# Spreading the second halves of crowded experts evenly over the units that have an empty half

## What is computed

```python
expert_id = g_top * MOE_PER_GROUP + top_i
gate = jnp.sum(jax.nn.one_hot(expert_id, MOE_EXPERTS, dtype=f32) * w[..., None], axis=1)
hid = jax.nn.silu(jnp.einsum('nd,edf->nef', hf, w_gate)) * jnp.einsum('nd,edf->nef', hf, w_up)
y = jnp.einsum('nef,efd->nd', hid * gate[:, :, None].astype(hid.dtype), w_down)
```

```
layer 0:  49 56 21 64  4 11 13 12 143 124 79 40 142 129 57 80
layer 1:  73 92 74 141 9  5  8  8  14  10 13 19  68 171 73 246
```

## Time and profile before

| | us |
|---|---|
| median of the three runs | 1496.72 |
| the profiled execution | 1495.05 |
| span of its trace | 1493.3 |
| TensorE matmul busy | 1313.4 (88%) |
| VectorE busy | 607.2 (41%) |
| ScalarE busy | 389.9 (26%) |
| GpSimd busy | 302.8 (20%) |

### The profile page before, as it was taken

How to read it: one execution, slowest core, us unless ns; L and a number is a source line. 1 busy time by engine, 2 the same in 40 slices (tenths; PEclk the granted TensorE clock), 3 DMA queues, 4 the chain that set the end, 5 groups by cost and what they waited for, 6 DMA issues and landing times.

```text
span 1493.3 us, 21495 instructions
## 1 busy us (share of the span) xinstructions
PE 1313.4 (88%) x7940; PEld 842.8 (56%) x7940; DVE 607.2 (41%) x1513; ACT 389.9 (26%) x815; POOL 302.8 (20%) x290
## 2 busy tenths in 40 slices
PE   4698999896996899998789999999999569779986
PEld 2345568665444666554635577766654356545546
DVE  3796671753143423111531004488841642301126
ACT  4204212213031121221320023477730411112212
POOL 5001200000010322332145592000000032223320
PEclk8789999798996699999899999899999859889998
DMA  8641522433159898986496573100002518979851
GB/s 228 218 160 21 95 59 84 143 126 100 57 189 344 326 335 293 341 291 222 164 107 151 175 247 123 47 2 2 2 3 82 225 47 302 393 318 328 297 191 57
DMA packets 129536, 257.36 MB, mean 172 GB/s; under 512 B 20184, under 2 KB 102476, under 8 KB 114445
## 3 DMA queue, kind: packets, MB, share of 16 engines
q1 hardware_dynamic: 98176, 188.76, 36.9%
q0 software_dynamic: 25296, 47.18, 12.1%
q10 hardware_dynamic: 5964, 20.07, 3.4%
HBM read 319.22 MB, written 22.55 MB: 229 GB/s over the span
## 4 chain that ended last, share of the span: by engine, by line
PE 76%; DVE 11%; DMA 5%; ACT 4%; issue 3%; POOL 1%; ACTq 0%; DVEq 0%; POOLq 0%
PE bank L833 14%; PE bank L535 13%; PE bank L715 7%; PE bank L851 7%; PE bank L523 4%; PE bank L974 3%; DMA arena<-in_e_w_up,arena 3%; PE bank L735 2%; PE bank L1002 2%; PE bank L986 2%; PE bank L822 2%; PE bank L658 2%; PE bank L912 2%; PE bank L469 2%; DMA arena<-in_ada_w 2%
## 5 line engine op out<-in xcount | busy, mean ns | idle before, releaser
L833 PE MATMUL bank<-arena 128*64 x1024 | 235.2, 389 | 18.3 <-DMA arena<-in_e_w_up,arena 18.3
L835 PE MATMUL bank<-arena 128*64 128x256 f32 x1024 | 235.8, 389 | 0.0
L535 PE MATMUL bank<-arena 128*128 128x512 f32 x448 | 199.0, 606 | 17.2 <-ACT arena L1082 10.2
L833 PEld LDWEIGHTS bank<-arena 128*64 128x64 f32 x1024 | 141.1, 140 | 91.9 <-issue 27.0
L535 PEld LDWEIGHTS bank<-arena 128*128 128x128 f32 x448 | 86.9, 195 | 125.1 <-issue 107.6
L835 PEld LDWEIGHTS bank<-arena 128*64 128x64 f32 x1024 | 140.8, 140 | 0.3 <-issue 0.2
L851 PE MATMUL bank<-arena 128*64 x256 | 118.4, 606 | 4.9 <-issue 4.9
L853 PE MATMUL bank<-arena 128*64 128x512 f32 x256 | 118.4, 606 | 0.0
L1996 DVE SCALAR_TENSOR_TENSOR arena<-bank,arena 128x256 f32<-128x256 f32 x32 | 15.5, 484 | 252.0 <-ACT arena L1294 252.0
L715 PE MATMUL bank<-arena 128*128 128x512 f32 x256 | 112.0, 593 | 1.5 <-ACT arena L1246 0.7
L2268 POOL MEMSET arena<- 128x4096 f32 x2 | 7.0, 3509 | 436.0 <-DVEq L1404 241.0
(11 more groups left out here) (475 smaller groups left out, 2255.4 us busy)
## 6 DMA issues: line engine op xcount, KB each, us to landing
arena<-in_ada_w SPq DMA_DIRECT2D x48, 1024.0 KB
arena<-in_e_w_gate SPq DMA_DIRECT2D x32, 1024.0 KB
arena<-in_e_w_up SPq DMA_DIRECT2D x32, 1024.0 KB
arena<-in_e_w_down SPq DMA_DIRECT2D x32, 1024.0 KB, 8.6
expert_rows<-arena ACTq DMA_DIRECT2D x30, 512.0 KB, 8.3
arena<-in_a_w_in SPq DMA_DIRECT2D x10, 1024.0 KB
arena<-in_n_w_in SPq DMA_DIRECT2D x10, 1024.0 KB
arena<-in_a_w_out SPq DMA_DIRECT2D x4, 1024.0 KB
```

Of the source, the lines that this page charges most:

```text
L535: last = mm(bank(stage, i)[:, :], chunk(kind, m, c)[:, k, j * P:(j + 1) * P], hT[:, k, :], start=(k == 0), stop=(k == KD - 1))
L833: mm(b[0:HS, CC * n:CC * n + CC], xgT[:, e % 2, k, 0:HS], w2[:, CC * k:CC * k + CC], start=(k == 0), stop=(k == KD - 1), skip_group_check= ...
L835: last = mm(b[HS:P, CC * n:CC * n + CC], xgT[:, e % 2, k, HS:P], chunk(w, l, e)[:, k, :], start=(k == 0), stop=(k == KD - 1), skip_group_c ...
```

## The change

The running number `Fi` of units with an empty half starts at 1 instead of 0, and both totals are read off: N units with an empty half, O further halves. Unit u takes a half where floor(Fi*O/N) grows by one, so the takers are spaced evenly, and the last unit with an empty half is always one of them. `Fi` then holds what the code behind it expects: the number of the further half for a unit that takes one, and 4096 and more for one that takes none. Nothing else is changed. By the counts above the takers become, in layer 0, units 3, 6 and 14 (before: 0, 1, 2), and in layer 1 units 5, 7, 9 and 11 (before: 4, 5, 6, 7). Their number stays, and so do the bytes.

```diff
-                link(V.tensor_tensor_scan(Fi, ones[:, 0:NE], fr, -1.0, ALU.mult, ALU.add))
-                link(V.scalar_tensor_tensor(out=Fi, in0=two, scalar=4097.0, in1=Fi, op0=ALU.mult, op1=ALU.add))
+                link(V.tensor_tensor_scan(Fi, ones[:, 0:NE], fr, 0.0, ALU.mult, ALU.add))
                 link(V.tensor_tensor_scan(Oi, ones[:, 0:NE], ov, 0.0, ALU.mult, ALU.add))
+
+
+                taken, whole, part = region(8832, [NE + 1]), region(8864, [NE]), region(8896, [NE])
+                link(V.memset(taken[:, 0:1], 0.0))
+                link(V.tensor_scalar(whole, jj[:, 1:NE + 1], Fi[:, NE - 1:NE], None, ALU.mult))
+                link(V.tensor_scalar(part, Fi, Oi[:, NE - 1:NE], None, ALU.mult))
+                link(V.tensor_tensor(sel, col(part), row(whole), ALU.is_ge))
+                link(V.tensor_reduce(taken[:, 1:NE + 1], sel, AX.X, ALU.add))
+                link(V.tensor_tensor(part, taken[:, 1:NE + 1], taken[:, 0:NE], ALU.subtract))
+                link(V.tensor_scalar(Fi, taken[:, 1:NE + 1], 4096.0, None, ALU.add))
+                link(V.scalar_tensor_tensor(out=Fi, in0=part, scalar=-4097.0, in1=Fi, op0=ALU.mult, op1=ALU.add))
```

## The result

The kernel after the change takes 1515.93 us (median of four runs, 1509.98 to 1517.12) against 1495.15 us before: a ratio of 1.0134, with a 95% interval of 1.0101 to 1.0167. It is 20 us slower. I had forecast 1500.0 us, with a range from 1483 to 1512. (The kernel before had a fourth execution beside it, so its median is 1495.15 and no longer 1496.72.) The profiled execution took 1517.12 us with a span of 1515.4, 22.1 us above that of before.

What follows compares the result with a forecast made beforehand. The prediction took TensorE as the bound, with two MoE waits in layer 1 for indirect up weights. Its terms, -23.3 + 22.8 + 3.8 = +3.3 us, gave 1500.0 us on a median of 1496.72, range 1483 to 1512.

Steps and rivals of the forecast that it cites:

- units 5 and 7 of layer 1, the old waits: Layer 1 MoE: TensorE's two waits for indirect up weights, with their clock loss, vanish: -23.3 us.
- lone takers 7, 9, 11 of layer 1: Layer 1 MoE: each lone taker in a short pitch costs 5.8 us, bounds 1.8 and 9.3; 17.4 us together.
- lone taker 14 of layer 0: Layer 0 MoE: 10.1 us available against 13.8 needed, a 3.7 us wait plus 1.7 of clock: 5.4 us.
- unit 6 of layer 0 and the one behind it: Layer 0 MoE: unit 6's gather is through in 11.5 us, costing nothing, at most 1 us.
- VectorE, both layers: Routing chain on VectorE: eight operations come, one goes, 1.9 us a layer unhidden; 3.8 us, bounds 3.5 and 4.2.
- have a pitch more than these and stay hidden behind the matmuls: MoE down gathers: one pitch more time than gate and up gathers, so no cost was counted.
- the 5.8 us at which I had put a late down gather: MoE: if the down gathers' cover went, each late one would cost up to 5.8 us, for 1.05 MB in company.
- The lone taker's wait: MoE, short pitch: built from unit 4 of layer 1, gather takes 13.8 us against 9.7 available, a 4.1 us wait.
- The clock loss: TensorE after an idle time runs partly at half clock: 1.7 us per lone taker, the smaller of 1.7 and 3.3.
- The value of before that I used to support them: Unit 7 of layer 1 before: 19.4 us from issue to matmul, less 5.8 for the down gather ahead, leaves 13.6.
- Rival 3: MoE queues don't drain between takers, so one taker's load runs into the next: +18.7 us, 1515 us; chance 20%.
- Rival 1: MoE lone takers wait little, 1.8 us x 3 and 1.4, without clock loss: -12.7, 1484 us; chance 25%.

Runs made afterwards that it cites:

- chain-only kernel: The changed kernel with the running number overwritten by the old formula, so new VectorE operations run but takers stay as before: 1497.58 against 1496.05 us, ratio 1.0013.
- the lone one at unit 7 of layer 0: Takers set by a list of ranks, layer 0 units 0, 1 and 7, layer 1 as before the change: 1508.76 against 1497.97 us, one execution each.
- the fastest kernel: The kernel before the change with GpSimd's order alone changed, gate and up gathers of unit e+1 ahead of unit e's down gather: 1483.10 us, ratio 0.9888.

## Why the prediction was wrong

By its own steps, in us; "measured" is the growth of the units' pitches between the two traces:

| step | forecast | measured |
|---|---|---|
| units 5 and 7 of layer 1, the old waits | -23.3 | -23.3 |
| lone takers 7, 9, 11 of layer 1 | 3 x 5.8 = 17.4 | 5.8 + 7.4 + 7.6 = 20.8 |
| lone taker 14 of layer 0 | 5.4 | 8.0 |
| unit 6 of layer 0 and the one behind it | 0, at most 1 | 0.5 + 9.6 = 10.1 |
| VectorE, both layers | 3.8 | 4.0 |
| sum | +3.3 | +19.6 |

- **What held.** The places and the kind of the waits: 7, 9, 11 and 14, for the indirect up weights, none at unit 5 (the pitch is 13.6), each followed by the low clock. The removed 23.3 us are all gone: unit 5 lost its wait altogether, and unit 7's has become that of a lone taker. The chain on VectorE is 0.1 us a layer longer than summed, since the two operations that read a scalar from the tile take 0.23 and not 0.17 us. (4.0 us is read from the traces; the chain-only kernel, with two operations more a layer, measured +2 us, -1 to +5.)
- **The step that failed** is the sentence that the down gathers "have a pitch more than these and stay hidden behind the matmuls". I checked the down gather against its own matmuls, which it never delayed. What it delayed was what stands behind it in GpSimd's queue: token rows and the empty gate and up gathers of the next unit, for which TensorE waits as well. Unit 7 waited 2.6 us for the one and 4.4 us for the other, and both waits went when the down gather moved nothing. I had listed the queue's order and had not asked who waits for that. It cost 9.6 of the 16.3 us that are missing (the 0.5 us of unit 6 itself lie within the 1 us that I had allowed), more than the 5.8 us at which I had put a late down gather.
- **Mis-sized terms.** The lone taker's wait was built from unit 4 and came out as 4.1 us (3.7 at unit 14); the four in the changed trace are 4.0, 5.5, 6.1 and 5.5, and the lone one at unit 7 of layer 0 7.4. From the issue of the gate gather to the first matmul I had 13.8 us; it took 13.8, 15.2, 15.9 and 15.7. That is 5.1 us of waiting too few. The clock loss was 1.5 to 2.5 us each, where I took the smaller of two values, 1.7: another 0.9. Together they are the 6.0 us by which these four terms fall short. The value of before that I used to support them, 13.6 us for the gather of unit 7, was 19.4 us less a term at the same 182 GB/s, and so no independent check. Why one lone taker waits 4.0 us and another 7.4 was not varied.
- **The rivals.** Rival 3 gave +18.7 us and 20% and came out on the number, but not by its mechanism. The queues do drain between takers: the pitch behind each taker of layer 1 is 11.8, and a lone taker with none since unit 1 pays the same as one in a row. Rival 1, faster, failed at unit 7 with the first 4.0 us.
- **What is left.** The two profiled executions differ by 22.1 us and the steps sum to 19.6. The changed one reaches the first changed instruction 3.1 us later already (481.47 against 478.41 us). Two kernels whose VectorE and TensorE code up to there is that of before are as late: TensorE starts on its lists at 485.45 us before, at 487.99 in the fastest kernel and at 488.40 in the one changed in layer 1 alone. So I take the 3 us as a difference between executions and not as an effect of the change.

The Trainium skill's page DMA: Bandwidth & Descriptors (Queues, rings and completion order) says that each DMA engine goes round-robin between the queues with work. From 592 to 598 us three queues had 50.0, 30.1 and 20.3% of the engines, so they do share them; whether in equal turns the shares do not tell. And sharing is only half of what a gather meets: for the first 4 us, from 588 to 592 us, GpSimd's queue had no bytes to move and SyncE took 1.68 MB (99.6% of the engines).

Open: why unit 6 of layer 1, behind the taker 5 that did not wait either, keeps its 11.8. There the pitch ahead is 13.6, in layer 0 it is 12.3. SyncE's next gate issue came 9.4 us after taker 5's down gather (1308.38 to 1317.77), and 8.1 us after taker 6's in layer 0 (587.97 to 596.04), so in layer 1 the empty gathers had more time before SyncE's weights; no run varied that alone. Nor was it shown which of the 16 engines was the last one with unit 7's packets.

## What to carry to other kernels

Spreading a load evenly is worth nothing by itself: first find the places where it is free. Here those were units 0 to 5, whose gathers run under a long start or beside extra TensorE work, as long as few of them in a row take, and the change moved two of layer 0's three takers out of them. When a transfer is checked for being hidden, check also everything behind it in its queue, down to the ones that carry no bytes but are waited for. And a late transfer is cheaper to cure where it is issued: a new order in GpSimd's program was worth 13 us, more than any placement of the load that was tried.

## What the hardware showed that I had not expected

- An indirect gather moved its first bytes some 4 us after its issue, and if SyncE's transfers were queued by then it got about half of the engines (1.26 of 2.52 MB from 592 to 598 us).
- Gathers with every index out of bounds are not free for a waiter: unit 7's, issued at 590.6 and 591.9 us behind a megabyte of down weights, held the matmuls until 608.8 us; from 600 to 604 us their queue moved 12 packets, beside 1.61 MB of SyncE's.
- An idle time of 4.0 to 6.1 us of TensorE cost 1.5 to 2.5 us more in the pitch than the wait itself, a quarter to nearly half as much again, with PEclk at 0.57 to 0.79 in the stretches over and behind it (0.79 from 1338 to 1346 us, behind the shortest).
